# Matrix-memory stage of a hybrid diffusion backbone: output products in units between the next head's scores, masks and gating on POOL, four decay buffers

## The reference

```python
def step(carry, inp):                       # one chunk, one direction
    b = jnp.cumsum(lfc, axis=-1)
    log_d = jnp.where(tri, b[..., :, None] - b[..., None, :] + igc[..., None, :], -jnp.inf)
    ...
    s = jnp.einsum('bhtd,bhsd->bhts', qc, kc) * jnp.exp(log_d - m_t[..., None])
    num = jnp.einsum('bhts,bhsd->bhtd', s, vc) + ...
    den = jnp.sum(s, axis=-1) + ...
    hc = num / jnp.maximum(jnp.abs(den), jnp.exp(-m_t))[..., None]

def merge_groups(a, hm, o, p):
    hm = jnp.swapaxes(hm, 1, 2) * jax.nn.sigmoid(o...)          # gate
    hm = head_layer_norm(hm, p['mlstm_norm'])                    # per head: (h - mean) / std
    return jnp.concatenate([rms_norm(a, p['attn_out_norm']), hm], axis=-1) @ p['w_out']
```

## Time and profile before

| | us |
|---|---|
| runs | 3295.4 (median), 3295.35, 3302.76 |
| profiled execution | 3296.22, span 3294.4 |
| PE busy | 3042.0 (92% of the span) |
| DVE busy | 1707.5 (52%) |
| ACT busy | 1020.0 (31%) |
| POOL busy | 282.6 (9%) |
| mean granted TensorE clock | 0.957 |

### The profile page before, as it was taken

One profiled execution on the slowest core, in us unless ns is written; L12 is line 12 of the kernel. 1 busy time (PEld: TensorE's weight loads), 2 busy tenths in 40 slices (PEclk: granted clock), 3 DMA queues, 4 the chain that ended last, 5 costly groups with the idle time before them and its releaser, 6 DMA issues.

```text
span 3294.4 us, 49682 instructions
## 1 busy us (share of the span) xinstructions
PE 3042.0 (92%) x18100; PEld 2858.5 (87%) x18100; DVE 1707.5 (52%) x3019; ACT 1020.0 (31%) x1720; POOL 282.6 (9%) x257
## 2 busy tenths in 40 slices
PE   6999999889898889999998999999988898889997
PEld 5999999879674779999998899999978765789997
DVE  4575565555247653455335566445555348543334
ACT  3212122433434442121124312212333434432233
POOL 2000000410000150000004100000320000500002
PEclk7999999999998989999999999999989999989999
DMA  6444443322100122244323344324322200423333
GB/s 200 129 121 127 115 140 110 101 68 58 54 1 1 45 84 63 76 123 116 88 64 103 90 128 139 98 84 140 102 80 58 61 1 1 116 82 102 87 94 109
DMA packets 454134, 293.22 MB, mean 89 GB/s; under 512 B 25974, under 2 KB 411356, under 8 KB 453980
## 3 DMA queue, kind: packets, MB, share of 16 engines
q1 hardware_dynamic: 453456, 291.01, 30.5%
q10 hardware_dynamic: 524, 0.18, 0.0%
HBM read 289.04 MB, written 2.10 MB: 88 GB/s over the span
## 4 chain that ended last, share of the span: by engine, by line
PE 81%; DVE 8%; issue 4%; ACT 4%; POOL 2%; DMA 1%; DVEq 0%; ACTq 0%; POOLq 0%; SPq 0%
PE ps L1678 24%; PE ps L1680 23%; PE ps L1679 23%; PE ps L2086 2%; DVE hn L1245 1%; DVE wsp L1157 1%; PE ps L2038 1%; POOL scr L707 1%; PE ps L2013 1%; PE ps L2014 1%; ACT wsp L775 1%; PE ps L2071 1%; ACT hn L805 1%; DVE ps L1238 1%; PE ps L2025 1%
## 5 line engine op out<-in xcount | busy, mean ns | idle before, releaser
L1678 PE MATMUL ps<-hn,wsp 128*128 128x384 f32 (+1 forms) x3200 | 1058.8, 331 | 58.4 <-DVE hn L1245 35.9
L1679 PE MATMUL ps<-hn,wsp 128*128 128x384 f32 (+1 forms) x3200 | 1047.5, 327 | 0.0
L1680 PE MATMUL ps<-hn,wsp 128*128 128x384 f32 (+1 forms) x3200 | 1046.9, 327 | 0.0
L1157 DVE TENSOR_TENSOR wsp<-raw,wsp 128x1024 fp32r<-128x1024 f32 x376 | 466.5, 1242 | 575.4 <-ACT wsp L775 575.3
L1678 PEld LDWEIGHTS ps<-hn,wsp 128*128 128x128 f32 x3200 | 613.5, 192 | 78.9 <-DVE hn L1245 35.6
L1679 PEld LDWEIGHTS ps<-hn,wsp 128*128 128x128 f32 x3200 | 614.5, 192 | 0.0
L1680 PEld LDWEIGHTS ps<-hn,wsp 128*128 128x128 f32 x3200 | 613.8, 192 | 0.0
L775 ACT ACTIVATE wsp<-raw 128x1024 fp32r<-128x1024 f32 x408 | 428.2, 1051 | 539.1 <-PE ps L1680 539.0
L1678 PE MATMUL ps<-aT,wsp 128*128 128x384 f32 (+1 forms) x1408 | 462.4, 328 | 29.5 <-DVE aT L1336 19.3
L1679 PE MATMUL ps<-aT,wsp 128*128 128x384 f32 (+1 forms) x1408 | 458.5, 326 | 0.0
L1680 PE MATMUL ps<-aT,wsp 128*128 128x384 f32 (+1 forms) x1408 | 458.3, 326 | 0.0
(11 more groups left out here) (212 smaller groups left out, 3049.3 us busy)
## 6 DMA issues: line engine op xcount, KB each, us to landing
modw<-in_w_mod SPq DMA_DIRECT2D x144, 512.0 KB, 4.2
raw<-in_ffn_w_gate SPq DMA_DIRECT2D x192, 256.0 KB, 3.4
raw<-in_ffn_w_up SPq DMA_DIRECT2D x192, 256.0 KB, 4.2
raw<-in_ffn_w_down SPq DMA_DIRECT2D x64, 448.0 KB, 3.4
raw<-in_w_in SPq DMA_DIRECT2D x96, 256.0 KB, 3.1
raw<-in_ffn_w_down SPq DMA_DIRECT2D x64, 256.0 KB, 4.2
raw<-in_w_out SPq DMA_DIRECT2D x64, 256.0 KB, 3.2
raw<-in_ffn_w_down SPq DMA_DIRECT2D x64, 192.0 KB, 3.6
```

The source lines that it names most:

```text
L1157: dve.tensor_tensor(wsp[:, cs, 1, 0:width], raw[:, slot, 0:width], wsp[:, cs, 0, 0:width].bitcast(F32), ALU.subtract).then_inc(wlo_done, 1)
L1678: pe.matmul(dst, w(0), x(0), start=first, stop=False)
L1679: pe.matmul(dst, w(0), x(1), start=False, stop=False)
L1680: return pe.matmul(dst, w(1), x(0), start=False, stop=last)
```

## The change

- PE does the output products of head h-1 during head h: unit 0 between head h's two gate broadcasts, unit 1 behind the scores of source tile 2, unit 2 behind those of tile 3, unit 3 behind those of tile 4. Head 3's four units stand alone at the end. DVE evacuates each unit behind the products of tiles 1, 2 and 3 (unit 0 ahead of tile 0).
- The diagonal mask is added on POOL (`gbc + mask`), and ACT adds `colF` as the bias of its exponential.
- `dbuf` gets a second pair (in `scr`), chosen by j's parity: a block may be written when the one four blocks earlier has been read.
- The evacuation has three small operations instead of four; in units 2 and 3 the product and the sum are one operation per token tile.
- Gate (`merge`) of heads 0 to 2 on POOL, between its masks for tile 4 and tile 5 of the next head; moments on DVE, a head later. Normalising of heads 0 to 2 on POOL; head 3's gate and normalising stay on DVE.

```diff
-                            if i >= 2:
-                                act.wait_ge(pb_done, i - 1)
+                            if i >= 4:
+                                act.wait_ge(pb_done, i - 3)
+                            decay = dbuf2[j % 2][:, d]
...
+            def matrix_memory(l):
+                tts = o_tts(l)
+                for h in range(MH):
+                    for j in range(NT):
+                        for d in range(2):
...
+                            pool.wait_ge(g_out, 4 * (MH * l + h) + 2 * d + 2)
+                            if i >= 4:
+                                pool.wait_ge(pb_done, i - 3)
+                            pool.tensor_tensor(
+                                dbuf2[j % 2][:, d, s], gbc[:, d, s], cst[:, C_MF + d * P:C_MF + (d + 1) * P], ALU.add
+                            ).then_inc(dg_done, 1)
+                        if h >= 1 and j == NT - 2:
+                            merge(l, h - 1)
+                pool.wait_ge(rs_done, l + 1)
+                for h in range(MH - 1):
+                    for tt in tts:
...
+                        pool.tensor_scalar(v, v, mv[:, k, 0:1], stat[:, 2, k:k + 1], ALU.subtract, ALU.mult
+                                           ).then_inc(fin_done, 1)
+            def merge(l, h):
...
+                pool.wait_ge(mo_out, out_unit_of(l, h, 3) + 1)
+                pool.tensor_tensor(g, g, hh[:, tts[0]:NT], ALU.mult).then_inc(merge_done, 1)
...
+                        if h >= 1 and OUT_AFTER[j] is not None:
+                            mlstm_out(l, h - 1, OUT_AFTER[j])
+                    if h >= 2:
+                        moments(l, h - 2)
+                last = MH - 1
+                mlstm_out(l, last, 0)
+                mlstm_out(l, last, 1)
+                moments(l, last - 1)
+                variances(l, 0, last)
+                mlstm_out(l, last, 2)
+                mlstm_out(l, last, 3)
+                dve.wait_ge(fstd_done, 3 * l + 2)
+                var = rs_of(l, 0, last)
+                dve.reciprocal(var, var).then_inc(rs_done, 1)
...
                 for h in range(MH):
-                    if h + 1 < MH:
-                        head_scores(h + 1)
-                    head_out(h)
+                    spread_gate(h, 0)
+                    if h >= 1:
+                        head_out(h - 1, 0)
+                    spread_gate(h, 1)
+                    for j in range(NT):
+                        source_scores(h, j)
+                        if h >= 1 and j >= 1 and OUT_AFTER[j - 1] is not None:
+                            head_out(h - 1, OUT_AFTER[j - 1])
+                for u in range(4):
+                    head_out(MH - 1, u)
```

More of the change, by code:

```diff
@@ L1519, in mixer @@
                                           stat[:, 1, 8 + k:9 + k], None, ALU.mult).then_inc(pv_out, 1)
[L1521 to L1530, removed]
-                                dve.wait_ge(pb_done, i - 1)
-                            dve.scalar_tensor_tensor(
-                                out=dbuf[:, d, s], in0=gbc[:, d, s],
-                                scalar=colF[:, j, 32 * d + h:32 * d + h + 1],
-                                in1=cst[:, C_MF + d * P:C_MF + (d + 1) * P], op0=ALU.add, op1=ALU.min
-                            ).then_inc(dg_done, 1)
+                for h in range(MH):
+                    if h >= 1:
+                        mlstm_out(l, h - 1, 0)
+                    for j in range(NT):
                         for d in range(2):
@@ new lines, in rs_of, with variances, moments @@
+            def rs_of(l, h1, h2):
+                t1 = o_tts(l)[0]
+                return stat[:, 2, 0:NT * MH].rearrange("p (h t) -> p h t", h=MH)[:, h1:h2, t1:NT]
+            def variances(l, h1, h2):
+                t1 = o_tts(l)[0]
+                var = mv[:, :, 1].rearrange("p (h t) -> p h t", h=MH)[:, h1:h2, t1:NT]
+                dve.tensor_copy(rs_of(l, h1, h2), var).then_inc(fvar_done, 1)
+            def moments(l, h):
+                if h < MH - 1:
+                    dve.wait_ge(merge_done, (MH - 1) * l + h + 1)
+                for i, tt in enumerate(o_tts(l)):
@@ new lines, in source_scores @@
+                def source_scores(h, j):
+                    if h > 0 or j >= 2:
+                        pe.wait_ge(pb_done, block_index(l, h, j, 0) - 2)
+                    if j == 0 and l < L - 1:
+                        for jj in range(NTC):
+                            pe.matmul(ps[:, 4, jj * CTX:(jj + 1) * CTX], qkT[:, MH + h, jj * P:(jj + 1) * P],
+                                      qkT[:, h, 0:CTX], start=True, stop=True)
+                    pe.matmul(ps[:, 2 + j % 2, 0:SEQ], qkT[:, MH + h, j * P:(j + 1) * P], qkT[:, h, CTX:T],
+                              start=True, stop=True).then_inc(s_done, 1)
@@ new lines, in head_out @@
+                def head_out(h, u):
+                    d, tts = u // 2, triples(l)[u % 2]
+                    slots = source_slots(l, d)
+                    o = out_unit_of(l, h, u)
+                    if o >= 3:
+                        pe.wait_ge(mo_out, o - 2)
+                    pe.wait_ge(pb_done, block_index(l, h, NT, 0))
+                    for m, tt in enumerate(tts):
+                        dst = ps[:, 5 + o % 3, m * (MDH + 1):(m + 1) * (MDH + 1)]
+                        src = sources_of(d, tt)
+                        for j in src:
+                            ins = pe.matmul(dst, pblk[:, h % 2, d, slots[j, tt]], vext[:, j, h],
+                                            start=j == src[0], stop=j == src[-1])
+                    ins.then_inc(mo_done, 1)
@@ L2104, in mixer @@
                         else:
-                            pe.wait_ge(fin_done, fin_before(l) + len(tts) * (cidx - HEADS + 1))
+                            h = cidx - HEADS
+                            if h < MH - 1:
+                                pe.wait_ge(fin_done, fin_before(l) + len(tts) * (h + 1))
+                            else:
+                                pe.wait_ge(fin_last, (NT if l else 0) + len(tts))
                         if i >= 4:
```

165 lines of the change are left out of this document (74 added, 91 removed).

## The result

The change made the kernel slightly slower: 3306.58 us median (3299.05 to 3309.57, 13 runs) against 3298.4 (3295.35 to 3302.76, 13 runs), ratio 1.0022, 95% interval [1.0014, 1.0031]. The forecast was 3275, with a range of 3263 to 3291, so it is wrong in sign. The profiled run of after took 3305.97 us with a span of 3304.2; before 3296.2 and 3294.4.

The account below looks back on a forecast made before the run. PE was taken to bind the program almost everywhere, with engines taking turns in this stage; gains of 17.8 us (layer 0) and 5.1 (layer 1), 22.9 less 2 for the clock, gave 3275.3 profiled, about 3275 median, range 3263 to 3291.

Parts of the forecast that it names:

- POOL's normalising: Heads 0 to 2 after the last product: 0.4 us per operation assumed, range 0.2 to 1.2, finished before the transposes.
- T0: Head 0's last product, timed from stage start: 13.1 us instead of 17.0 in layer 0, a gain of 3.2 in layer 1.
- six heads at full clock: Heads 1 to 3 of both layers: 69.6 us in layer 0 (gain 0.4), 60.0 in layer 1 (loss 8.0).
- wait for unit 1: In each later head of layer 0, DVE waits 2.8 us for PE's unit 1, its longest wait in a head.
- the line: POOL's two-input additions priced at 0.33 + 0.0020 us per column: mask 0.58, gate 1.87 in layer 0, 1.35 for 512 columns.
- rival 1: POOL slower than its assumed price: gates and masks doubled, normalising at 1.16 us and late, 36.5 us in all, 3311; chance 0.07.
- Rival 4: PE's order makes DVE wait longer at each unit, another 3 us a head, 18 us, giving 3293; chance 0.08.
- three signs of being wrong: A mask over 1 us, heads of layer 1 staying above 22 us, or first transposes of head 2 waiting for POOL.
- From this I take 2 for the clock: 2 us off the 22.9 gain, for unit 0 and gate broadcast at 0.50 after PE's rest at head ends in layer 0.
- rival 2: PE's clock falls in every head, some 2.5 us in each of six, 15 instead of 2, giving 3288; chance 0.13.
- done at 20.2: Layer 0's end: POOL's eighteen normalising operations start at 13.0, take 7.2 us; transposes need head 2's tiles at 21.6.
- T3: Time of head 3's last product, from which the end of the stage is counted: 20.0 us in layer 0, 15.4 in layer 1.

Follow-up runs that it names:

- e1: Changed kernel with the gate of heads 0 to 2 on POOL placed behind the last tile's masks instead of ahead of them: 3278.8 us, ratio 0.9944 to before.
- e3: Changed kernel with normalising of heads 0 to 2 back on DVE, behind the statistics of head 3: 3301.0 us, ratio 1.0002 to before.
- e5: Changed kernel with the edits of e1 and e3 together: 3273.8 us, ratio 0.9923 to before.
- e2: Changed kernel plus three unused 128x512 matmuls on PE ahead of unit 0, gate left where it was: 3296.2 us, ratio 0.9988 to before.
- e6: e5 with each head's moments on DVE ahead of the next unit instead of behind the last products: 3273.5 us, ratio 0.9911 to before.
- e8: e5 plus two unused 128x512 matmuls on PE ahead of each head's unit 0: 3275.2 us, ratio 0.9931 to before.
- e10: e5 plus one unused 128x512 matmul ahead of unit 0, in layer 0 only: 3275.0 us, ratio 0.9922 to before.
- e11: e10 plus 28 and 16 unused 128x128 matmuls in PE's two rests at the end of the stage: 3268.9 us, ratio 0.9914 to before.
- e9: e8 plus 56 and 32 unused 128x128 matmuls in PE's two rests at the end of the stage: 3293.3 us, ratio 0.9968 to before.

## Why the prediction was wrong

The places were right, and two prices were not: that of the clock and that of POOL's normalising. Against the profiled execution the forecast was 30.7 us too low. By its own terms, measured in after:

| step | predicted | measured | short by |
|---|---|---|---|
| T0, layers 0 and 1 | 13.1, 13.55 | 13.7, 13.9 | 0.9 |
| six heads at full clock | 69.6 + 60.0 | 3 x 24.05 + 3 x 20.63 | 4.4 |
| clock in the heads | 2 in all | 4.3 + 1.3, 2.4 + 3.6 | 9.6 |
| clock in the tails | 0 | 2.6, 2.4 | 5.0 |
| POOL's normalising | 0 | 6.1, 3.4 | 9.5 |

Sum 29.4; about 1 more lies outside the stage. The clock in the heads is each head's length above head 1's, which ran at full clock; the clock in the tails is after's less e1's, which issue the same but for the place of head 2's gate; POOL's share is e1's tail less the one predicted (20.0 + 7.5 and 15.4 + 6.1, the second terms being what w_out stood behind DVE's last normalising operation before). That last share is what remains, but the forecast's own terms give the same. In layer 0 the eighteen take 14.70 us where 7.2 were reckoned, 7.5 more, and there were 1.4 to spare (20.2 for 21.6): 6.1. In layer 1 the twelve take 9.80 for 4.8, with 1.5 to spare (15.2 for 16.7): 3.5. With the eighteen on DVE (e3, e5) 2.3 and 1.2 of it come back, since there they take 4.7 us of the path themselves.

**T0 and the heads at full clock: right within 5%.** For T0 that is partly luck: nine of the eleven experiments' traces have 15.0 or 15.1 in layer 0, and in layer 1 it is 13.9 only because the clock fell, 11.9 at full clock. The wait for unit 1 was 2.53 us (2.8 said), and PE's rest at a head's end 3.70 (3.6 said). Masks and gates cost less than the line. Of rival 1 the half on two-input work is out; its other half, normalising that comes late (8.4 us where it said 12.3), came true, and so did its outcome. Rival 4 is out. Two of the three signs of being wrong that the forecast named appeared: heads of layer 1 above 22 us, and transposes of head 2 that wait for POOL.

**The step that failed first is "From this I take 2 for the clock".** I saw the rest of 3.6 us and had the earlier trace rows, in which the clock stood at 0.50 for 6 us behind such a stretch, and priced only unit 0 and the gate broadcast (up to 1.7, once). What runs at 0.50 is everything up to the first product: unit 0, the broadcast, four passes of context scores, four of scores, 10.7 us; head 2 lost 4.3. It fell in four heads of six and at the start of both tails; where I took off 2, it cost 11.6 us in the heads and 5.0 in the tails. That is rival 2, which had 15 for it, and to which I gave 0.13 on the ground that a window with PE busy for 17.4 of 19.8 us stood at 1.00. That window's mean said nothing of the gap inside the head to come: PE's longest rest in it was 0.93 us, and the new heads of that layer end in rests of 2.89 and more. The old heads 2 and 3 of layer 0 did have rests, 2.87 and 1.63 us with 1.1 of work between, and the clock fell behind them. e1 and e2 show it from two sides, one taking most of the rest away, the other filling it.

**The second is "done at 20.2".** With 0.4 a piece this held; at the measured 0.828, inside my own range of 0.2 to 1.2, the eighteen end at T3 + 30. DVE released them at 15.3 and not 13.0, with PE's units at half clock for 5.2 us behind T3. I kept both ends of the price but worked the upper one out only in rival 1 (at 1.16, 12.3 us late), tied there to double prices for gates and masks as well and given 0.07. By itself it is 13.0 + 21.6 = 34.6, 13 us late, so the range was too narrow at its slow end. And 0.4, MEMSET's neighbourhood, was the wrong row to be near: it costs 1.8 times a two-input mask of the same size (0.828 against 0.455).

**The sentence on the Trainium skill** (GPSIMD Engine Reference, Engine selection) now has its rows: two-input masks on POOL 0.455 against DVE's 0.345, closer than twice; one-input normalising 0.82 from start to start (14.70 for 18) against DVE's 0.26 (4.70 for 18), a factor of three where the page says near line rate. Had the page been believed for the price, the sum and its error would have been the same.

**What the change is worth when its order is mended.** e5's stage is 24.2 us shorter than before's, and the forecast was 22.9 without the clock. That agreement is luck. Against the forecast e5's six heads are 7.6 us shorter (67.4 and 54.6 for 69.6 and 60.0), its tails 6.0 longer (31.3 and 23.7 for 27.5 and 21.5), T0 1.9 longer and 1.7 shorter; and it is another kernel, with the gate behind the masks and the normalising on DVE. What it does show: the loss isn't in doing the output products in units. Most of it is in a gate of 1.8 us ahead of two masks (e1), a smaller part in POOL's normalising (e3, e5).

**Open.** Why the clock falls in one head and not in another that looks the same. In after the rests ahead of unit 0 of heads 2 and 3 in layer 0 are 3.70 and 3.71 us; behind the first the clock stood at 0.50 through 10.7 us of work and 4.3 us were lost, behind the second for some 3 us, and 1.3 were lost. In e5 the rest ahead of unit 0 is 0.90 us at the ends of heads 1 and 2 of layer 0, and only behind the first did it fall (e1 and e6 show the same); unused matmuls ahead of it held it in e8, e10 and e11. At the start of layer 1's stage it falls in some kernels' profiles and not in others' of nearly equal instructions (T0 13.9 or 11.9), which moves 2 us; in layer 0 it is the same (15.0 or 13.7). Among e5 and its variants the three with 13.9 in layer 1 (e6, e9, e10) also have a fall right behind T3 there, and the three with 11.9 (e5, e8, e11) have none. No run separates these.

## What to carry to other kernels

When work moves to an in-order engine, put the piece that nobody waits for behind the pieces that somebody does: here 1.8 us ahead of two 0.45 us masks turned a change worth 0.56% (e1) into a loss of 0.22%. Where a change brings TensorE a new rest, price the rest and, as the slow end of the range, all of its work at half clock up to the next wait for another engine; rests of 3.7 us cost 4.3 and 1.3 us in this way here. Look at the gap itself, not at the busy share of a long window. Where the price of an operation isn't in the trace, work the whole sum at both ends before the range is written.

## What the runs showed of the hardware that was not expected

- The granted clock stayed at 0.50 for 10.7 us in which TensorE was busy 10.64, after it had rested 3.7 us.
- It fell behind a rest of 0.90 us too (e5, layer 0):

```profile
1024.00:1030.00 6.00, 5.10 (x20) 3.54 (x19) 3.26 (x12) 0.98 (x2) 2.22 (x2) 0.78 0.00 0
1030.00:1036.00 6.00, 6.00 (x10) 2.94 (x10) 0.54 (x2) 4.26 (x11) 1.28 (x3) 0.50 0.00 0
```

- and matmuls whose product nobody reads held it at 1.00 (e10, same place):

```profile
1024.00:1030.00 6.00, 6.00 (x33) 3.78 (x32) 3.42 (x12) 2.18 (x5) 3.10 (x4) 1.00 0.00 0
1030.00:1036.00 6.00, 4.89 (x18) 2.54 (x17) 3.04 (x10) 4.34 (x11) 1.76 (x5) 1.00 0.00 0
```

- The same rest of 3.7 us was followed in the next head by only some 3 us at 0.50.
- On POOL a subtraction and multiplication with two per-partition scalars takes 0.828 us for 128x128, an addition of two tensors of that size 0.455.
